# Hybrid flow step with expert retrieval: token tile 4 ranked last, gathered rows dealt between all ranking items

## The reference

```python
q = (xt @ w_query).reshape(t, PEER_HEADS, 2, PEER_KEY_DIM // 2)
s = jnp.einsum('thpd,hpkd->thpk', q, sub_keys)
s_half, i_half = lax.top_k(s, 16)                  # 8 heads x 2 halves x 128 keys
cand = s_half[:, :, 0, :, None] + s_half[:, :, 1, None, :]
top_s, top_pos = lax.top_k(cand, 16)               # 16 of 256, as (i, j) of 128 x 128 experts
gates = softmax(top_s)
a = gelu(einsum('tkd,td->tk', expert_u[es], xs))   # 8 heads x 16 = 128 experts per token
y = einsum('tk,tkd->td', gates * a, expert_v[es])
```

## Time and profile before

| | us |
|---|---|
| median of 3 runs (lowest, highest) | 1929.65 (1924.39, 1934.65) |
| the profiled execution, own time | 1945.27 |
| its span in the trace | 1943.5 |
| mean granted TensorE clock | 0.97 |

### The profile page before, as it was taken

How to read it: one execution, slowest core, us unless ns; L and a number is a source line. 1 busy time by engine, 2 the same in 40 slices (tenths; PEclk the granted TensorE clock), 3 DMA queues, 4 the chain that set the end, 5 groups by cost and what they waited for, 6 DMA issues and landing times.

```text
span 1943.5 us, 21544 instructions
## 1 busy us (share of the span) xinstructions
PE 1795.4 (92%) x8020; PEld 1152.3 (59%) x8020; DVE 1292.2 (66%) x2593; ACT 293.5 (15%) x661; POOL 896.7 (46%) x837
## 2 busy tenths in 40 slices
PE   4988898998999999998999999996889999999994
PEld 1666743554444359987888888884554444444441
DVE  2110476989579699998998975568875623336767
ACT  0120010555100001111111100005550000000000
POOL 1010225665456324334455555668865665435540
PEclk9999999999999999998999999998999999999998
DMA  8895859888999977559999999999989999999995
GB/s 360 338 370 214 344 160 394 291 286 324 392 324 363 390 272 298 187 192 362 366 361 375 386 387 409 405 394 329 327 308 409 409 409 409 409 409 409 409 410 203
DMA packets 168441, 670.21 MB, mean 345 GB/s; under 512 B 19563, under 2 KB 19691, under 8 KB 163085
## 3 DMA queue, kind: packets, MB, share of 16 engines
q0 software_dynamic: 112512, 410.79, 56.2%
q1 hardware_dynamic: 51072, 242.25, 31.8%
q10 hardware_dynamic: 4752, 15.81, 2.1%
HBM read 659.27 MB, written 7.39 MB: 343 GB/s over the span
## 4 chain that ended last, share of the span: by engine, by line
PE 46%; DMA 18%; DVE 18%; POOL 11%; issue 6%; ACT 1%; ACTq 0%; DVEq 0%; another core or an unknown queue 0%; POOLq 0%
PE psum L966 19%; POOL arena L566 11%; DMA arena<-in_expert_u_dram,arena 9%; DMA arena<-in_expert_v_dram,arena 4%; DVE arena L1511 4%; PE psum L751 4%; PE psum L992 3%; PE psum L995 3%; DVE psum L1784 3%; PE psum L740 2%; PE psum L1029 2%; DVE arena L1707 2%; DMA arena<-in_w_ada_dram 2%; PE psum L1006 2%; PE psum L1004 2%
## 5 line engine op out<-in xcount | busy, mean ns | idle before, releaser
L566 POOL DMA_INDIRECT arena<-in_expert_u_dram,arena x384 | 468.5, 1220 | 386.0 <-DVE arena L1511 261.6
L1511 DVE CUSTOM_DVE_ANT_0 arena<-arena 128x1024 f32<-128x1024 f32 x384 | 461.0, 1222 | 182.1 <-DMA arena<-in_expert_u_dram,arena 153.0
L566 POOL DMA_INDIRECT arena<-in_expert_v_dram,arena x384 | 390.7, 1018 | 357.9 <-DVE psum L1784 175.9
L1784 DVE SCALAR_TENSOR_TENSOR psum<-arena,psum 128x1024 f32<-128x1024 f32 x254 | 327.0, 1287 | 193.2 <-DMA arena<-in_expert_v_dram,arena 165.0
L893 PE MATMUL psum<-arena 128*128 128x256 f32 x2048 | 446.0, 381 | 7.3 <-DMA arena<-in_expert_uT_dram 7.3
L966 PE MATMUL psum<-arena 128*128 128x512 f32 x1024 | 443.7, 594 | 1.6 <-DMA arena<-in_expert_v_dram 1.6
L893 PEld LDWEIGHTS psum<-arena 128*128 128x128 f32 x2048 | 390.8, 191 | 61.3 <-issue 7.6
L966 PEld LDWEIGHTS psum<-arena 128*128 128x128 f32 x1024 | 193.3, 190 | 253.0 <-issue 249.0
L1064 PE MATMUL psum<-arena 128*128 128x128 f32 x1280 | 148.9, 278 | 2.1 <-DVE arena L1668 1.4
L1064 PEld LDWEIGHTS psum<-arena 128*128 128x128 f32 x1280 | 147.1, 194 | 3.6 <-issue 1.9
L1324 ACT ACTIVATE arena<-psum 128x512 f32<-128x512 f32 x64 | 38.2, 597 | 379.7 <-PE psum L893 292.6
(11 more groups left out here) (188 smaller groups left out, 1410.1 us busy)
## 6 DMA issues: line engine op xcount, KB each, us to landing
arena<-in_expert_uT_dram SPq DMA_DIRECT2D x128, 512.0 KB
arena<-in_expert_v_dram SPq DMA_DIRECT2D x128, 512.0 KB
arena<-in_w_ada_dram SPq DMA_DIRECT2D x12, 2048.0 KB
arena<-in_w_in_dram SPq DMA_DIRECT2D x11, 2048.0 KB
arena<-in_w_query_dram SPq DMA_DIRECT2D x8, 2048.0 KB, 22.7
arena<-in_w_in_dram SPq DMA_DIRECT2D x30, 512.0 KB, 7.9
arena<-in_w_o_dram SPq DMA_DIRECT2D x4, 2048.0 KB
arena<-in_expert_u_dram,arena POOLq DMA_INDIRECT x384
```

Source lines behind the costliest of these rows:

```text
L566: pool.indirect_dma_start(slot, None, table[0], bass.IndirectOffsetOnAxis(ap=number, axis=0)).then_inc(land, 16)
L1511: dve.tensor_tensor_reduce(UR[b], UR[b], U2B[e], 1.0, 0.0, ALU.mult, ALU.add, DOTS[e % 2][:, k:k + 1]).then_inc(u_free, 1)
L1784: dve.scalar_tensor_tensor(ys, row, weight, ys, ALU.mult, ALU.add).then_inc(v_free, 1)
```

## The change

- The dense tiles keep their numbers, but tile 4 is now ranked and routed last: `ORDER` is 0, 1, 3, 2, 4. Its raw key scores are kept in the columns of UT that belonged to tiles 0 and 1 (`late_scores`), its digits in AF and BF, its gates in GATE[1]. The last 24 blocks of expert_u are read in a rotated order, so that the gelus which land on ranking's buffers come last; ACT waits for tile 4's routing at pairs 56 and 60 instead of for tile 2's at pair 52.
- Tile 4's digits are turned on PE after the last dense score (`spread(ORDER[-1])`), and the first `hot` waits for that.
- `DOTS_AFTER` now names 25 items, from item 0 on, and the groups run on from tile 1 into tile 2 (`score_next`); only three of the 28 groups ahead of the gates stand behind the items. `SCORED_GROUPS` goes from 10 to 12, so four groups of tile 2 are left for the value stage.
- `U2B[2]` shares its place with `U2B[1]`, so POOL loads it only when tile 1's last row has been scored, behind tile 2's first eight fetches.
- The late rounds stand behind blocks 18, 21, 26, 32, 39, 43, ... 68. In `late_rounds` a round's fetch now stands ahead of the value rows of the same step. The pacing of the last 80 value rows starts at block 68 instead of 76.
- The finish of tile 0 stands behind item 3 instead of item 9; the places of gate exponents and spreads on PE and ACT follow the new order.

```diff
-ORDER = (0, 1, 3, 4, 2)
+ORDER = (0, 1, 3, 2, 4)
...
-        U2B = [at(47104, D), at(44032, D), at(47104, D)]
+        U2B = [at(47104, D), at(44032, D), at(44032, D)]
...
-        HOT_J = [at(44032, BATCH, NKEYS), UT[:, :, 3 * P:4 * P]]
+        HOT_J = [at(47104, BATCH, NKEYS), UT[:, :, 3 * P:4 * P]]
...
+        def late_scores(e, qg):
+
+            if e == ORDER[-1]:
+                return UT[:, 2 * qg:2 * qg + 2, 0:2 * P]
+            return LATE[e][:, qg, :].rearrange("p (a b) -> p a b", a=2)
+
+        def scored_block(n):
+
+            i = n - KEYHALF - UPPER_PARTS
+            return n if i < 0 else KEYHALF + UPPER_PARTS + (i + 16) % 24
...
                 for k in range(0, BESIDE, 4):
+                    r = GATE_ROUNDS + 2 + k // 4
+                    if r < ROUNDS:
+                        pool.wait_ge(summed, r - 1)
+                        sum_fetch(r)
                     if k < GROUP:
                         pool.wait_ge(ring_out, NKEYS + 20 + 4 * k)
                     pool.wait_ge(v_free, HK + k + 4)
                     fetch(expert_v, EID[0][:, k:k + 4], VR[2], v_land, k % GROUP)
-                    r = GATE_ROUNDS + 2 + k // 4
-                    if r < ROUNDS:
-                        pool.wait_ge(summed, r - 1)
-                        sum_fetch(r)
...
             routed(2)
+            score_rows(2, 0, GROUP)
+            pool.wait_ge(u_free, GROUP + 2 * HK)
             pool.dma_start(U2B[2], u2_d[2 * P:3 * P, :]).then_inc(late_u2_in, 16)
-            score_rows(2, 0, GROUP * SCORED_GROUPS)
+            score_rows(2, GROUP, GROUP * SCORED_GROUPS)
...
-                if m == (KEYHALF + UPPER_PARTS) // 2:
-                    act.wait_ge(pick_step, PICKED[2])
+                if m == (KEYHALF + UPPER_PARTS) // 2 + 4:
+                    act.wait_ge(pick_step, PICKED[4] - PICKS_OF[4] + ROUTE_AT[3])
+                if m == (KEYHALF + UPPER_PARTS) // 2 + 8:
+                    act.wait_ge(pick_step, PICKED[4] - PICKS_OF[4] + ROUTE_AT[5])
...
+                if i == 0:
+                    dve.wait_ge(spread_done, len(DENSE))
                 dve.wait_ge(spread_out, d + 1)
...
+            def score_next(count):
+
+                for r in range(scored_rows[0], scored_rows[0] + count):
+                    if r == HK:
+                        dve.wait_ge(q_done, 4 * TILES)
+                        dve.memset(COLUMNS, 0.0).then_inc(zero_set, 1)
+                        dve.wait_ge(late_u2_in, 16)
+                    if r == HK + GROUP * WEIGH_AFTER:
+                        weigh(1)
+                    score(1 + r // HK, r % HK, r % HK + 1)
+                scored_rows[0] += count
...
                 if n in DOTS_AFTER:
-                    score(1, k, k + GROUP * DOTS_AFTER[n])
-                    k += GROUP * DOTS_AFTER[n]
+                    score_next(GROUP)
+            score_next(HK + GROUP * SCORED_GROUPS - scored_rows[0])
...
-SPREAD_AT = {8: 3, 24: 4}
-EXPONENTS_AT = {3: 3, 18: 4, 35: 2}
+SPREAD_AT = {15: 3}
+EXPONENTS_AT = {11: 3, 32: 2, 55: 4}
...
-DOTS_AFTER = {3: 1, 5: 1, 7: 1, 9: 1, 11: 1, 13: 1, 15: 1, 17: 1, 19: 1, 21: 1, 22: 1, 23: 1, 25: 1, 27: 1, 29: 1}
-FINISH_AT, DEVIATION_AT, STORE_AT = 9, 8, 32
-NUMBERS_AT, WEIGH_AT, WEIGH_AFTER, WEIGHTS_AT = 26, 41, 2, 50
-SCORED_GROUPS, GATE_ROUNDS = 10, 20
+DOTS_AFTER = (0, 1, 2, 3, 5, 7, 9, 10, 11, 12, 13, 15, 16, 17, 18, 19, 20, 21, 22, 23, 24, 25, 26, 27, 28)
+FINISH_AT, DEVIATION_AT, STORE_AT = 3, 6, 32
+NUMBERS_AT, WEIGH_AT, WEIGH_AFTER, WEIGHTS_AT = 26, 42, 3, 54
+SCORED_GROUPS, GATE_ROUNDS = 12, 20
 BESIDE = ROUND * (ROUNDS - GATE_ROUNDS)
-ROUND_AFTER = {(33 + 2 * n if n < 2 else 38 + 17 * (n - 2) // 4): GATE_ROUNDS + n for n in range(ROUNDS - GATE_ROUNDS)}
+LATE_STEPS = (18, 21, 26, 32) + tuple(39 + 17 * n // 4 for n in range(ROUNDS - GATE_ROUNDS - 4))
+ROUND_AFTER = {n: GATE_ROUNDS + i for i, n in enumerate(LATE_STEPS)}
```

More of the change, by code:

```diff
@@ L217, in backbone @@
         EQ = [at({0: 14336, 1: 28672}.get(e, 45056), PEER_HEADS, CAND) for e in range(TILES)]
-        LATE = {e: at(o, 4, HALF) for e, o in ((1, 26624), (3, 35840), (4, 37888), (2, 39936))}
+        LATE = {e: at(o, 4, HALF) for e, o in ((1, 26624), (3, 37888), (2, 39936))}
         VR = [UR] + [[at(26624 + 1024 * i, D) for i in range(GROUP)]] * (TILES - 1)
-        U2B = [at(47104, D), at(44032, D), at(47104, D)]
+        U2B = [at(47104, D), at(44032, D), at(44032, D)]
         X1B = [at(1024, D)] + [at(37888 + 1024 * (e - 1), D) for e in range(1, TILES)]
@@ L521, in _ @@
                 if n < NKEYS:
-                    src = expert_uT[n]
+                    src = expert_uT[scored_block(n)]
                 else:
@@ L929, in spread @@
                 pe.wait_ge(pick_step, PICKED[e])
+                if e == ORDER[-1]:
+                    pe.wait_ge(rank_out, 2)
                 for i, src in enumerate((DIGITS[e][0], DIGITS[e][1], DGATE[e])):
@@ L1086, in _ @@
                 expert_scores(m)
+            spread(ORDER[-1])
             for i in range(BATCHES):
@@ L1289, in keep_scores @@
                             act.wait_ge(store_out[0], 80)
-                        act.activation(LATE[e][:, i % 4, :], bank(2 + i % 2), ACT.Copy).then_inc(ss_out, 1)
+                        act.activation(late_scores(e, i % 4), bank(2 + i % 2).rearrange("p (a b) -> p a b", a=2), ACT.Copy
+                                       ).then_inc(ss_out, 1)
                 for i in range(4 * tiles[0], 4 * tiles[-1] + 4):
@@ L1376, in _ @@
                 expert_gelu(m)
+            take_spread(ORDER[-1])
             for i in range(BATCHES):
@@ L1693, in rank_keys, with scored @@
                     dve.wait_ge(topk_step, 20 * si)
-                sc = LATE[e][:, qg, :] if e else bank(2 + si % 2)
+                def scored(c):
+                    if e:
+                        return late_scores(e, qg)[:, c // 2, c % 2 * P:(c % 2 + 1) * P]
+                    return bank(2 + si % 2)[:, c * P:(c + 1) * P]
                 def best(c, lo):
@@ L1701, in rank_keys @@
                     for c in range(4):
-                        src = sc[:, c * P:(c + 1) * P] if lo == 0 else SW[:, c, :]
+                        src = scored(c) if lo == 0 else SW[:, c, :]
                         dve.max(VAL[:, best(c, lo)], src).then_inc(topk_step, 1)
@@ L1709, in rank_keys @@
                         for c in range(4):
-                            dve.match_replace(SW[:, c, :], VAL[:, best(c, 0)], sc[:, c * P:(c + 1) * P], LOWEST
+                            dve.match_replace(SW[:, c, :], VAL[:, best(c, 0)], scored(c), LOWEST
                                               ).then_inc(topk_step, 1)
@@ L1873, in _ @@
             dve.wait_ge(u2_in, 16)
-            k = 0
-            for n, (do, e, part) in enumerate(
-                    [(rank_keys, 3, qg) for qg in range(4)] + [(route, 3, part) for part in range(PARTS)]
-                    + [(rank_keys, 4, qg) for qg in range(4)] + [(route, 4, part) for part in range(PARTS)]
-                    + [(rank_keys, 2, qg) for qg in range(4)] + [(route, 2, part) for part in range(PARTS)]):
+            scored_rows = [0]
+            def score_next(count):
[8 more added lines that the diff above has]
+                scored_rows[0] += count
+            steps = []
+            for e in ORDER[2:]:
+                steps += [(rank_keys, e, qg) for qg in range(4)] + [(route, e, part) for part in range(PARTS)]
+            for n, (do, e, part) in enumerate(steps):
                 do(e, part)
```

16 lines of the change are left out of this document (4 added, 12 removed).

## The result

The change makes the kernel slower: 1952.51 us as a median of 4 runs (1948.36 to 1959.24) against 1929.94 us for the kernel before (4 runs), a ratio of 1.0122 with the interval 1.0099 to 1.0145. Forecast were 1925.3 us and a range up to 1939. The profiled execution took 1959.24 us with a span of 1957.4.

What follows compares the result with a forecast made beforehand. PE was taken to bound the score and value stages, with DMA full too in the value stage. Terms -9.4 + 13 + 3 - 9.4 - 1.6 = -4.4 us, applied to the 1929.65 us median, gave 1925.3; range 1908 to 1939.

Steps and rivals of the forecast that it cites:

- Step 1: Dense scores: 224 rows scored by 1307, ahead of PE's end at 1312.8, so the gates start at about 1314.3: -9.4 us.
- the cadence: Rows ahead of the gates, one group per item: 16.4 us per group, 2.05 per row, over 196 rows: 402 us.
- the hole: Between tile 1's and tile 2's rows, at the new load of U2B: the gather queue idles about 9 us.
- Step 2: The gates: as many steps, rounds and rows as before, so 0 us.
- Step 3: Value stage, first late round, behind block 18: PE waits for rows, +13 us, bounds 11.5 to 18.7.
- Step 4: Value stage, fifth late round, behind block 39: PE waits for rows, +3 us, bounds 0 and +6.
- step 5: The end: 14.2 us behind PE's last block instead of 23.6, -9.4, and PE's wait at 1911.08 goes, -1.6.
- The waits for tile 4's routing: ACT's waits in the dense scores, binding at PE's pair 60, about 1285; rows done by about 1215: costed at nothing.
- B: Dense scores: gathers fall short of the gates; at 380 GB/s gates shift +6, sum +11, 1941 us; chance 0.14.
- A: Value stage: the late rounds don't hold PE, everything else as forecast; -20.4 us, 1909; chance 0.27.
- C: The end stays bound by gathers, so its 9.4 us are not gained; +5 us, 1935; chance 0.14.

Runs made afterwards that it cites:

- steps 5 earlier: The kernel before with its first two late rounds behind blocks 28 and 30 instead of 33 and 35; ratio to the kernel before 1.0077.
- the early load: The changed kernel with a second copy of tile 2's input loaded early into a free column, read by tile 2's first 16 rows; ratio to the kernel before 1.0057.
- single fetches: The changed kernel with the rows of tiles 1 and 2 fetched one by one instead of by four; ratio to the kernel before 1.0019.
- the second run: The changed kernel, unaltered, measured and profiled again in a second series; ratio to the kernel before 1.0102.
- the row-by-row kernel of before: The kernel before with the rows of tiles 1 and 2 fetched one by one, nothing else changed; ratio to the kernel before 0.9942.
- three twelve-group kernels: The changed kernel with late rounds moved back (1.0037), also with tile 2's input loaded early (0.9994), and also with rows fetched one by one (0.9960).
- the kernel with all three edits: The changed kernel with tile 2's input loaded early, rows fetched one by one and late rounds moved back; ratio to the kernel before 0.9960.
- ten groups: The changed kernel with ten groups of tile 2 ahead of the gates instead of twelve, late rounds as before; ratio to the kernel before 0.9959.
- eleven with the early load: The changed kernel with eleven groups, tile 2's input loaded early, late rounds behind 29, 32, 36 and from 40; ratio to the kernel before 0.9926.

## Why the prediction was wrong

Its own sum was -4.4; the traces give +13.9, which is 18.3 us more. On top of that, it applied the difference to the median as if both profiled executions stood alike to theirs. They did not: that of before was 15.3 us above its median, that of after 6.7. These 8.6 us more close the gap of 27. Where the profiled execution of before lost them can be seen only in part: its first row was scored at 859, while the run with steps 5 earlier, which is the same kernel up to there, scored it at 853.

*Step 1, 224 rows by 1307: wrong, and the step that failed.* G came at 1328.3, 14 us late; the last row was scored at 1327, 20 us late. Piece by piece: the 28th row came at 901 instead of 894 (+7; no run shows why). Rows 28 to 128 took 222 us instead of 212 (+10): 2.2 each where the cadence of the earlier trace rows gave 2.05. The hole before tile 2's first row was 19 us instead of 11 (+8), and the last 95 rows took 185 instead of 190 (-5). These two belong together, since eight rows lay ready behind the hole: with the early load all rows came to 8 to 10 us less, so the 9 us that the forecast had put down for the hole were about right.

So the term that was mis-sized is the cadence. Three lines of the kernel before show what it was made of (the last is a window, with the columns of the earlier trace rows):

```profile
1048.23 1.68 POOL L566 DMA_INDIRECT arena<-in_expert_u_dram,arena  x1 [10.26 <-DVE arena L1511]
...
1063.85 1.23 DVE L1511 CUSTOM_DVE_ANT_0 arena<-arena 128x1024 f32<-128x1024 f32 x1 [1.17 <-DMA arena<-in_expert_u_dram,arena]
...
1043.31:1076.17 32.86, 32.86 (x155) 28.88 (x154) 28.79 (x97) 2.61 (x5) 19.81 (x16) 1.00 0.93 358
```

The first of its two groups waited for no row: all eight had been fetched beforehand, and POOL stood 10.3 us with no buffer free. Only the second waited for rows, and its step took 18.6 us, 2.3 per row. At the start of the stretch eight rows lay ready, at its end four (the third group waits from its fifth row on), so some 12 rows landed in the time in which 16 were scored. The mean of 16.4 per group hides that, and it was carried over 196 rows. What it asks for can be worked out as an estimate: a row of 0.524 MB every 2.05 us and a block every 3.45 are 256 + 152 = 408 GB/s. The stretch itself carried 358, and the changed kernel 384 from 894 to 1300. With single fetches rows 28 to 128 took 211 to 213 us, the forecast's 212. So the 2.05 could be had, but not with fetches by four and an item between the groups.

*Step 2, the gates:* +1.3, or -0.9 in the second run, for 0. PE's first one-hot products took 6.26 us behind its long wait, against 4.78 in the row-by-row kernel of before.

*Step 3, PE's wait behind block 18: right*, 12.2 and 12.1 us for 13 (bounds 11.5 to 18.7). *Step 4, behind block 39:* 7.4 for 3, above its upper bound of 6. The working assumed 7.7 to 9.3 us from the last issue to landing; it took 12.1 (1614.28 to 1626.39). After 46.5 idle microseconds POOL issued all it owed at once, and 413 GB/s were carried from 1615 to 1632; that the full queue made the landing late is the likely reading, not one that a run tests. That idle time was in the order that I had read, and I did not ask what it would do.

*Left out:* the clock behind a wait, 1.7 and 1.5 us. And PE's waits and the pacing did what *step 5* said and more: T + 10.9 for T + 14.2, since DVE could start tile 3 at T - 6.8 (1939.67) where the forecast had T - 3.4. In the three twelve-group kernels in which PE doesn't wait for late rounds, the end is 12.3 to 14.8, about as forecast.

*The waits for tile 4's routing, costed at nothing: right.* PE was busy in every microsecond from 900 to 1300 in the changed kernel.

*The rivals.* B is what happened to step 1: it named 394 GB/s as the deciding point and, at 380, a gate start at about +6 and a sum of +11. Measured were 384 GB/s, +4.6 and +13.9. It was given 0.14, because the forecast believed one cadence over the average of the two halves of the stage that stood in the same rows. Its mechanism holds for the gathers as they were issued, not as a limit of the engines: the kernel with all three edits carried 400 and met the gates. By the Trainium skill (DMA: Bandwidth & Descriptors, "Where 436 GB/s comes from") a load from HBM is bound by about 358 GB/s per core; from that figure the forecast estimated 1356 for the start of the gates. The runs carried 384 to 400 GB/s over 406 us and the latest G is 1330.7, so none bears it out. A and C fell: PE did wait, and the end was not bound by gathers.

## What to carry to other kernels

Moving work ahead of a deadline helps only up to the point where it is still early. Compare both arrivals in the trace (who waited for whom, and how long) before adding more: here ten groups left DVE 16 us early, eleven with the early load were even, twelve were 18 to 26 us late. A rate that was read over a short stretch which starts with its buffers full is no rate for a long one; work out the average that a plan needs, and set it against the average of the whole stage, not of its best part. And where gathers recycle a few slots, look at how they are issued, and at what stands between them in the queue, before dealing the work anew: cutting the fetches from four rows to one made the kernel before 0.6% faster, where the change as it stands cost 1.2%.

## What the runs showed of the hardware

- After a pause of 7 to 12 us PE ran the next 3.5 us near half clock: 16 matmuls took 3.64 and 3.42 us instead of 1.92, granted clock 0.50 and 0.55. Shorter pauses did it too: one of 3.4 us in the kernel before with steps 5 earlier was followed by 6.2 us at 0.50, and one of 2.45 us in the kernel before (1449.71) by a round of 3.52 us at 0.53.
- A gather that lands in 7.7 us with an empty queue took 12.1 as the eighth of a row of fetches issued back to back, with the block stream beside them (1614.28 to 1626.39).
- The 16 DMA engines were told busy to 0.99 or more at 384, 395 and 400 GB/s alike. A share near 1 doesn't say that no more can be carried.
- PE's dense scores began anywhere from 850 to 872 us, by 9 us even in two executions of the same kernel, while the first row of the changed kernels was scored between 835 and 844. Two chains that race to one point must be timed each from its own start.
